# Second mixer: the values' projection by seven half-size products, and the second modulation summed by adding transfers

## The reference, cut to what matters

```python
c_act = silu(c)
mod = c_act @ ada_w[layer] + ada_b[layer]         # six rows of 1024; the change touches rows 2 to 5 of one layer
proj = h @ hy_w_in                                # 256 x 1024 by 1024 x n
v = proj[:, HY_V:HY_V + 1024]                     # the values' projection: four chunks of 256 columns
y = ssd_chunked(x, dt, A, B, C)                   # the scan, 32 heads
```

## Time and profile before

| what | value |
| --- | --- |
| median of three runs | 1464.32 us |
| lowest, highest | 1462.7, 1465.55 us |
| span of the profiled execution | 1458.9 us |
| PE busy | 1373.3 us, 94% |
| DVE busy | 873.2 us, 60% |
| ACT busy | 252.0 us, 17% |
| POOL busy | 258.8 us, 18% |
| moved from HBM | 352.58 MB, 243 GB/s over the span |

### The profile page before, as it was taken

One profiled execution on the slowest core, in us unless ns is written; L12 is line 12 of the kernel. 1 busy time (PEld: TensorE's weight loads), 2 busy tenths in 40 slices (PEclk: granted clock), 3 DMA queues, 4 the chain that ended last, 5 costly groups with the idle time before them and its releaser, 6 DMA issues. The chain is left out here.

```text
span 1458.9 us, 18939 instructions
## 1 busy us (share of the span) xinstructions
PE 1373.3 (94%) x7533; PEld 1013.0 (69%) x7533; DVE 873.2 (60%) x1502; ACT 252.0 (17%) x540; POOL 258.8 (18%) x342
## 2 busy tenths in 40 slices
PE   5999999887766999999999999999999999999997
PEld 1877655554433788868888888777776878888843
DVE  2458685442222668763454685788763874777864
ACT  2221121000001211222345101000002113211101
POOL 5078010000000200453355402100020100000000
PEclk9999999998998999999999999999999999999999
DMA  9976878999999598856774455898864552555531
GB/s 350 319 258 229 283 307 347 363 416 415 417 418 378 181 316 277 298 162 164 161 179 132 158 163 175 326 336 311 303 230 141 155 157 80 163 164 171 172 129 46
DMA packets 176055, 355.57 MB, mean 244 GB/s; under 512 B 7289, under 2 KB 137040, under 8 KB 158560
## 3 DMA queue, kind: packets, MB, share of 16 engines
q1 hardware_dynamic: 166720, 313.64, 60.6%
q0 software_dynamic: 9248, 40.71, 9.5%
HBM read 352.58 MB, written 1.74 MB: 243 GB/s over the span
## 5 line engine op out<-in xcount | busy, mean ns | idle before, releaser
L1824 PE MATMUL PS<-HT,ring 128*128 128x256 f32 x1152 | 258.3, 382 | 0.1
L1824 PEld LDWEIGHTS PS<-HT,ring 128*128 128x128 f32 x1152 | 215.4, 190 | 36.0 <-issue 7.9
L1542 DVE TENSOR_TENSOR X<-X,PS 128x1024 f32<-128x1024 f32 x14 | 17.1, 1221 | 112.0 <-PE PS L1318 112.0
L1265 PE MATMUL PS<-ring_extra,slot_rows 128*32 128x256 f32 x576 | 55.2, 440 | 27.7 <-DMA ring_extra<-in_expert_w_gate 7.0
L2758 PE MATMUL PS<-HT,ring 128*128 128x256 f32 x352 | 76.8, 379 | 0.0
L2787 PE MATMUL PS<-ada_stage,half_sums 128*128 128x256 f32 x320 | 75.6, 379 | 0.0
L2787 PE MATMUL PS<-ring,half_sums 128*128 128x256 f32 x320 | 75.6, 379 | 0.0
L2758 PEld LDWEIGHTS PS<-HT,ring 128*128 128x128 f32 x352 | 66.7, 190 | 9.0
L2764 PE MATMUL PS<-ring,hid 128*128 128x512 f32 x160 | 71.8, 592 | 0.0
L2787 PE MATMUL PS<-ring,HT 128*128 128x256 f32 x304 | 68.8, 379 | 0.0
L2787 PEld LDWEIGHTS PS<-ring,half_sums 128*128 128x128 f32 x320 | 59.4, 190 | 11.2 <-issue 4.3
(11 more groups left out here) (713 smaller groups left out, 2450.5 us busy)
## 6 DMA issues: line engine op xcount, KB each, us to landing
ring<-in_hy_w_in SPq DMA_DIRECT2D x40, 1024.0 KB, 7.5
ring_extra<-in_w_ada SPq DMA_DIRECT2D x24, 1024.0 KB, 8.0
ada_stage<-in_ada_w POOLq DMA_DIRECT2D x24, 1024.0 KB, 7.4
ring<-in_ffn_w_gate SPq DMA_DIRECT2D x22, 1024.0 KB, 5.8
ring<-in_ffn_w_up SPq DMA_DIRECT2D x22, 1024.0 KB, 5.7
ring<-in_ffn_w_down SPq DMA_DIRECT2D x22, 1024.0 KB, 6.0
ring_extra<-in_expert_w_down SPq DMA_DIRECT2D x18, 1024.0 KB, 22.9
ring_extra<-in_expert_w_up SPq DMA_DIRECT2D x18, 1024.0 KB, 20.1
```

What stands on the lines that cost most here:

```text
L1265: mm = pe.matmul(PS[e * SLOTS:(e + 1) * SLOTS, 2, j * CW:(j + 1) * CW], hs[:, k, e * SLOTS:(e + 1) * SLOTS], w[e][:, k, :], start=(k == 0) ...
L1542: dve.tensor_tensor(part, part, PS[:, 6:8, :], ALU.add).then_inc(added, 1)
L1824: mm = pe.matmul(dst, w[:, k, half * P:(half + 1) * P], HT[:, k, :], start=(k == 0), stop=(k == KT - 1))
```

## The change

- The 14 sums and two products on DVE are taken out (`add`). ACT multiplies each piece with its scalar instead (`weigh`, one 128 x 2048 instruction at step `a + 2`, last quarter): the first two into `acc`, the other 14 in place. GpSimd then issues, at the next step's first quarter, a transfer from the piece's buffer to `acc` that adds to what stands there (`accum_op=ALU.add`), so 14 transfers of 1 MB inside the core's memory.
- There are two buffers (`stages`) instead of one. SP's load of piece `a` is issued one step earlier than before; from piece 4 on it waits until the adding transfer of piece `a - 2` has landed.
- The values' four chunks are taken in two pairs. A pair is a 2 x 2 block product done with seven half-size products (P1 to P7, each four 128 x 128 by 256 products with half the depth) in place of eight. PE's slots are the same quarters; the eighth quarter of a pair is empty. DVE makes four sums of `HT` (`v_half`, steps 8 to 11), four sums of weights per pair (`v_sum`, steps 14 to 18, 128 x 1024 each) and joins seven results per pair (`v_join`, 128 x 256 each). ACT moves P1 in place of emptying the four chunks.
- A pair's two weight slots come free after P7 and P4. PE waits for both chunks of the pair at its start, for the sums, and in step 20 for the last join. `gate_rows` waits for the last adding transfers.
- Several semaphores of earlier stages are used again with offsets, `dt_parts` is put into another buffer, and the load of `gate_a` waits for the small loads; none of this changes an amount of work.

```diff
-        stage = sb(scope, "ada_stage", [P, 2 * D])
+        stages = sb(scope, "ada_stage", [P, 2, 2 * D])
+        stage = stages[:, 0]
...
-        add_at = {(s, 3): s - 2 for s in range(2, 18)}
+        weigh_at = {(s, 3): s - 2 for s in range(2, 18)}
         QUARTERS = [(s, q) for s in range(NP + 1) for q in range(4)]
+
+        V_ORDER = ("P2", "P1", "P3", "P5", "P6", "P7", "P4")
+        V_BANKS = ((2, 3, 6), (0, 1, 7))
+        V_HOMES = {"P2": (0, 0), "P1": (0, 1), "P3": (1, 0), "P5": (1, 1), "P6": (2, 0), "P7": (0, 0), "P4": (2, 1)}
+        v_halves = BC[:].rearrange("p a s -> p (a s)").rearrange("p (j k n) -> p j k n", j=4, k=4)
+        v_sums = ((out_sum0[:, 0], out_sum0[:, 1], out_sum0[:, 2]),
+                  (carve(rx_zb, 0, [4, CW]), out_sum0[:, 0], out_sum0[:, 1]))
+        v_half_at = {(8 + j, 3): j for j in range(4)}
+        v_sum_at = {(14, 3): (0, 0), (15, 1): (0, 1), (15, 2): (0, 2), (15, 3): (0, 3),
+                    (16, 1): (1, 0), (17, 2): (1, 1), (17, 3): (1, 2), (18, 1): (1, 3)}
+        v_join_at = {(V0 + 2 * pair + at // 4, at % 4): (pair, at) for pair in range(2) for at in (3, 5, 6, 7)}
+
+        def v_product(s, q):
+            return divmod(4 * (s - V0) + q, 8)
+
+        def v_home(pair, name):
+            bank, at = V_HOMES[name]
+            return PS[:, V_BANKS[pair][bank], at * CW:(at + 1) * CW]
+
+        def v_done(pair, name):
+            return 5 * pair + V_ORDER.index(name) + 1
+
+        def evacuated(s):
+            return s + 1 if s < V0 else s + 1 - (Q0 - V0)
...
-                    for (step_no, _), a in add_at.items():
-                        if step_no == s + (s > 0) or (s == 0 and step_no <= 1):
-                            if a:
-                                sp.wait_ge(summed, a)
-                            sp.dma_start(stage[:].rearrange("p (a n) -> p a n", a=1), wv[:, ds(a // 2, 1), 1 + a % 2, :])\
-                                .then_inc(fetched, 16)
+                    for (step_no, _), a in weigh_at.items():
+                        if step_no == s + (2 if s else 0) or (s == 1 and step_no == 2):
+                            if 2 <= a < 4:
+                                sp.wait_ge(weighed, a - 1)
+                            elif a >= 4:
+                                sp.wait_ge(summed[a % 2], 16 * (a // 2 - 1))
+                            sp.dma_start(stages[:, a % 2:a % 2 + 1, :], wv[:, ds(a // 2, 1), 1 + a % 2, :])\
+                                .then_inc(fetched[a % 2], 16)
                             fetched_n += 1
...
+                def v_seventh(pair, at):
+
+                    n = base + V0 + 2 * pair
+                    if at == 0:
+                        arrive(pe, n)
+                        arrive(pe, n + 1)
+                        if pair:
+                            pe.wait_ge(evac, evacuated(V0 - 1))
                         else:
-                            mm = pe.matmul(dst, w[:, k, half * P:(half + 1) * P], HT[:, k, :],
-                                           start=(k == 0), stop=(k == KT - 1))
-                    return mm
+                            pe.wait_ge(cb_mv, SSM_G)
+                            pe.wait_ge(v_summed, 4)
+                    name = V_ORDER[at]
+                    if name == "P5":
+                        pe.wait_ge(v_summed, 4 + 4 * pair + 1)
+                    if name == "P6":
+                        pe.wait_ge(xready, SSM_IN // CW)
+                        pe.wait_ge(v_summed, 4 + 4 * pair + 2)
+                    if name == "P7":
+                        pe.wait_ge(v_summed, 4 + 4 * pair + 4)
+                        pe.wait_ge(v_joined, 3 * pair + 1)
+                    if name == "P4":
+                        pe.wait_ge(v_joined, 3 * pair + 2)
+                    w0, w1, (t1, t2, t4) = w_slot(n), w_slot(n + 1), v_sums[pair]
+                    a11, a12, a22 = HT[:, 0:4, 0:P], HT[:, 4:8, 0:P], HT[:, 4:8, P:S]
+                    lhs, rhs = {"P1": (a11, w0[:, 0:4, :]), "P2": (a12, w0[:, 4:8, :]), "P3": (v_halves[:, 3], w1[:, 4:8, :]),
+                                "P4": (a22, t4), "P5": (v_halves[:, 0], t1), "P6": (v_halves[:, 1], t2),
+                                "P7": (v_halves[:, 2], w1[:, 0:4, :])}[name]
+                    for k in range(4):
+                        mm = pe.matmul(v_home(pair, name), lhs[:, k, :], rhs[:, k, :], start=(k == 0), stop=(k == 3))
+                    mm.then_inc(used if name in ("P7", "P4") else v_products, 1)
...
+                        pair, at = v_product(s, q)
+                        if at < len(V_ORDER):
+                            v_seventh(pair, at)
+                    else:
+                        if q == 0:
+                            arrive(pe, base + s)
+                            if s in (Q0, Q0 + 1):
+                                pe.wait_ge(v_joined, 6)
+                            elif s >= 2:
+                                pe.wait_ge(evac, evacuated(s - 2))
+                        mm = quarter(s, q)
+                        if q == 3:
+                            mm.then_inc(used, 1)
...
-                        pe.wait_ge(summed, ADDS)
+                        pe.wait_ge(v_joined, 3)
+                        for j in range(2):
+                            pe.wait_ge(summed[j], 16 * (KT - 1))
...
+                def weigh(a):
+                    j, k = a % 2, a // 2
+                    act.wait_ge(fetched[j], 16 * (k + 1))
+                    if a == 0:
+                        act.wait_ge(cv_ok, 1)
+                    act.activation(acc[:, j, :] if k == 0 else stages[:, j, :], stages[:, j, :], ACT.Copy,
+                                   scale=cv[:, k:k + 1]).then_inc(weighed, 1)
...
+                    if V0 <= s < Q0 and v_product(s, q)[1] == 2:
+                        pair = v_product(s, q)[0]
+                        act.wait_ge(v_products, v_done(pair, "P1"))
+                        act.activation(V[:, 1, 2 * pair * CW:(2 * pair + 1) * CW], v_home(pair, "P1"), ACT.Copy)\
+                            .then_inc(v_moved, 1)
...
+                    if (s, q) in weigh_at:
+                        weigh(weigh_at[s, q])
...
-                def add(a):
-                    j, k = a % 2, a // 2
-                    dve.wait_ge(fetched, 16 * (a + 1))
-                    if a == 0:
-                        dve.wait_ge(cv_ok, 1)
-                    if k == 0:
-                        dve.tensor_scalar(acc[:, j, :], stage[:], cv[:, 0:1], None, ALU.mult).then_inc(summed, 1)
+                def v_half(j):
+                    if j == 0:
+                        dve.wait_ge(cb_ps, SSM_G)
+                        dve.wait_ge(n_left, 4)
+                        dve.wait_ge(n_right, 4)
                     else:
-                        dve.wait_ge(summed, a - 1)
-                        dve.scalar_tensor_tensor(out=acc[:, j, :], in0=stage[:], scalar=cv[:, k:k + 1], in1=acc[:, j, :],
-                                                 op0=ALU.mult, op1=ALU.add).then_inc(summed, 1)
+                        dve.wait_ge(v_summed, j)
+                    a11, a12, a21, a22 = (HT[:, 4 * h:4 * h + 4, i * P:(i + 1) * P] for i in range(TT) for h in range(2))
+                    at, in0, in1, op = ((0, a21, a22, ALU.add), (2, a11, a21, ALU.subtract),
+                                        (1, v_halves[:, 0], a11, ALU.subtract), (3, a12, v_halves[:, 1], ALU.subtract))[j]
+                    dve.tensor_tensor(v_halves[:, at], in0, in1, op).then_inc(v_summed, 1)
+
+                def v_sum(pair, j):
+                    n = base + V0 + 2 * pair
+                    w0, w1, (t1, t2, t4) = w_slot(n), w_slot(n + 1), v_sums[pair]
+                    if j == 0:
+                        for item in (n, n + 1):
+                            dve.wait_ge(landed[slots[item]], 16 * turns[item])
+                    else:
+                        dve.wait_ge(v_summed, 4 + 4 * pair + j)
+                    if pair and j in (1, 3):
+                        dve.wait_ge(v_products, v_done(0, "P5" if j == 1 else "P6"))
+                    out, in0, in1 = ((t1, w1[:, 0:4, :], w0[:, 0:4, :]), (t2, w1[:, 4:8, :], t1),
+                                     (w1[:, 0:4, :], w1[:, 4:8, :], w1[:, 0:4, :]), (t4, w0[:, 4:8, :], t2))[j]
+                    dve.tensor_tensor(out, in0, in1, ALU.subtract).then_inc(v_summed, 1)
+
+                def v_join(pair, at):
+                    v00, v01, v10, v11 = (V[:, i, (2 * pair + h) * CW:(2 * pair + h + 1) * CW] for i in range(TT) for h in range(2))
+                    if at == 3:
+                        dve.wait_ge(v_moved, pair + 1)
+                        dve.tensor_tensor(v00, v_home(pair, "P2"), v10, ALU.add).then_inc(v_joined, 1)
+                    if at == 5:
+                        dve.wait_ge(v_products, v_done(pair, "P6"))
+                        dve.tensor_tensor(v11, v_home(pair, "P6"), v10, ALU.add).then_inc(v_joined, 1)
```

(45 more changed lines are left out.)

36 lines of the change are left out of this document (18 added, 18 removed).

## The result

The changed kernel takes **1498.28 us** (median of 4, 1496.03 to 1499.01) against 1464.93 beside it: ratio 1.0232, 95% interval 1.0212 to 1.0252. So it is 33 us slower; forecast were 17, and 1498 lies past the top of the range, 1495. The profiled execution took 1497.79 us, with a span of 1495.8. In every execution on record time and span are 1.6 to 2.1 us apart, so the 5.4 us between the span before (1458.9) and the median are for the most part a profiled execution faster than the median; between the two spans the loss is 36.9 us.

The account below looks back on a forecast made before the run. PE was taken to bound the kernel, with the transfers next. Span 1458.9 - 3.65 (fewer products) + 21 (adding transfers) = 1476.3, plus 5.4 from span to median, forecast 1481 us; range 1460 to 1495.

Parts of the forecast that it names:

- Part 1: Values' projection: seven products for eight, 16 records fewer at 0.228 us, 3.65 us off PE, all on the path.
- Part 2: Values' sums and joins on DVE, steps 15 to 19: 42.3 us against PE's 44.8, hidden by lag, costed at nothing.
- Rival (b): Steps 17 to 20: transfers fit, but PE waits for DVE and its joins; gain gone, 1464 us; chance 0.10.
- Part 3: Modulation on ACT: 16 products at 1.9 us, 30 us fit; a piece may be some 10 us late before PE stops.
- Part 4: Adding transfers, steps 5 to 16: twelve need 52 us against 31 of room, so PE loses 21 us.
- The cost: Queue time of one adding transfer: between 2.5 and 5.1 us, taken as 4.3 with some overlap of read and write.
- The room: Time for adding transfers in steps 5 to 16: 21 us free of 87, plus 10 of lateness, 31 us.
- the 10 us of lateness: How late a modulation piece may land, about two steps less ACT's work, before PE stops: some 10 us.
- (a): An adding transfer costs what a load does, 2.5 to 3 us; PE waits 0 to 5 us, 1460.7 us; chance 0.30.
- (c): An adding transfer takes 8 us and more, queues adding row by row; PE loses 65 us, 1526 us; chance 0.05.
- The clock: PE's clock should stay at its upper level, since waits of 2 to 3 us a step did not lower it elsewhere.
- What was said to show it: Steps 7 to 17: PE waits behind evacuations, ACT at `weigh`; DMA share 0.97 and more; adding transfers land in 7 to 12 us.

Follow-up runs that it names:

- experiment 2: The changed kernel with its 14 adding transfers taken out and the modulation's sums left out, ACT's products and seven-product values kept: 1460.52 us, ratio 0.9979 to before.
- experiment 4: The changed kernel with the values' projection by full products, so the modulation's move alone: 1498.2 us, ratio 1.0234 to the kernel before.
- Experiment 3: The kernel before with the seven-product values alone, all 16 pieces still multiplied and summed by DVE with one buffer: 1471.27 us, ratio 1.0048.
- Experiment 8: A separate program computing nothing of the reference: 1 MB copies and adding transfers alone, six at once, and four beside eight loads; six copies 17.9 us, six adding 32.5.
- experiment 9: The changed kernel with 17, 6 and 12 idle products before PE's waits in steps 11, 13 and 15: 1500.27 us, ratio 1.0236 to the kernel before.

## Why the prediction was wrong in size, and where right

**Part 1** was sized right. From the traces, one execution each (the first stretch runs from the mixer's start to the start of step 20):

| kernel | steps 0 to 19 | step 20 to the end |
| --- | --- | --- |
| before | 162.96 us | 814.44 us |
| changed | 196.52 us | 816.09 us |
| experiment 2, no transfers | 159.51 us | 816.10 us |
| experiment 4, full products | 201.65 us | 814.05 us |

Without the transfers steps 0 to 19 lose 3.45 us for the 3.65 forecast. But "the 3.65 us arrive whole" holds for the mixer only: some 1.65 us go again behind it, where PE gets the wait for `hid_rows`. The prediction had no term for that.

**Part 2** held: among PE's new waits in the mixer none has DVE as its releaser, neither at P7 and P4 nor at step 20. Rival (b) falls by that and by experiment 2. Experiment 3 shows that it was near: had DVE kept four of its sums in steps 14 to 17, it would have been the bound.

**Part 3** held: 2.00 us a product, 1.9 taken. The chain from a late piece over ACT's evacuations and, later, the exponentials to PE is what the waits show.

**Part 4, the step that failed: not the mechanism, but the size of both its terms,** the cost of a transfer and the room for it. The forecast was a loss of 21 us; the changed kernel loses 37 against the one without transfers.

The cost: the bounds were 2.5 and 5.1 us and I took 4.3, allowing that reads overlap writes. Experiment 8 gives 5.1: the upper bound, without overlap, 1.95 times a copy (5.06 / 2.59). 12 x (5.1 - 4.3) = 9.6 us.

Beside loads the ratio comes out alike: 12 transfers in 33.0 us are 2.75 each, and eight at that price leave 21.2 of the 43.2 us to the four adding ones, 5.3 each, 1.93 times 2.75. The Trainium skill's "Collectives: The Full Stack", The bandwidth ceiling, states a measured ratio of 1.93 between a copy and a reduce, and gives two source reads on the same ring as the reason. The ratio agrees with this run; the reason no run here shows. The estimate of 4.8 us that the prediction worked out from that page was nearer than its 4.3.

The room: with 5.1 in place of 4.3 the sum is 1464.3 - 3.65 + 12 x 5.1 - 31 = 1490.9, and some 7 us are missing. Going from no transfers to adding ones cost (1.0232 - 0.9979) x 1464 = 37 us and to copies (1.0052 - 0.9979) x 1464 = 11 us; with demands of 61 and 31 that leaves a room of 24 and 20 us, where I took 31. Experiment 4, against before, leaves 27. Part of it can be the rate: at the 2.75 us of experiment 8, the 25.78 MB take 67.6 us and 19.4 of 87 are free, not 21. How the remainder divides between that and the 10 us of lateness is not settled.

The loop checks it another way: two pieces and two chunks at 2.6 us and two adding transfers at 5.1 are 20.6 us of the queues for two steps, against periods of 20.1 to 22.3.

**Rivals (a) and (c)** fall by experiment 8: not 2.5 to 3 us, and not 8.

**The clock.** "Should stay at its upper level" was wrong: it is 0.89 over 560 to 680 us. The waits that I had looked at were shorter than I said: 2.0 us in the whole of 895 to 960 us, not 2 to 3 us a step. Behind its four waits of 4.4 to 8.2 us PE comes back at the lower level (16 records in 6.54 us behind the longest); behind the one of 3.2 us, in step 13, it does not (3.69 us, and 1.00 in the window of 590 to 600 us). In steps 11 and 15 the lower level costs nothing that experiment 9 could see; for the waits at the scan weights from step 16 on it was not tried.

**What was said to show it** came: waits behind ACT's evacuation, ACT waiting at `weigh`, a DMA share of 1, landing in 10.6 us.

## What to carry to other kernels

Sum the queues' time of each stage before work is moved from an engine to transfers, and count a transfer that adds as two; a full stage pays with every load in it. Take a room that is worked out from a stage's share and rate as an upper bound: 31 us on paper were 20 to 27. Here the useful half of the change wanted only a second buffer, and the old sums done up to four steps earlier.

## What the runs showed of the hardware

- An adding transfer of 1 MB within SBUF takes 5.1 us of the 16 queues for a copy's 2.6, or 7.2 us against 4.9 alone, and its issue holds POOL for 0.86 us against 0.53.
- The rate misleads beside it. Windows of experiment 8, six copies and then six adding transfers: the share is 0.92 and 1.01, at 370 and 203 GB/s. 203 GB/s over 31 us are 6.3 MB, six pieces, so the view counts the bytes of an adding transfer once.

```profile
93.00:110.00 17.00, 0.00 (x0) 2.66 (x6) 1.00 0.92 370
111.00:142.00 31.00, 0.00 (x0) 4.71 (x6) 1.00 1.01 203
```

- After a wait of 8.24 us PE ran 16 records in 6.54 us and not 3.72, and the window of 570 to 580 us has a granted clock of 0.62; with idle products ahead of it and a wait of 1.96 us, the same 16 took 3.72 us (experiment 9).
